# Expert tokens fetched as quarter rows and transposed on VectorE, stores of the residual stream moved into the router stage

## The reference

```python
h = rmsnorm(x, g_pre_ffn) * (1 + sc2) + sh2
aff = softmax(h @ w_router)                    # 16 experts
g, idx = lax.top_k(aff.T, cap)                 # cap = 64 latent tokens per expert, 16 context tokens
xe = h[idx]
hid = silu(xe @ w_gate[e]) * (xe @ w_up[e])    # 1024 -> 2816
ye = (hid @ w_down[e]) * g[..., None]          # 2816 -> 1024
out = zeros.at[idx].add(ye)
x = x + gt2 * rmsnorm(out, g_post_ffn)
```

## Time and profile before

| | us |
|---|---|
| median of three runs | 2022.64 (2022.20 to 2023.88) |
| profiled execution, its own time | 2023.81 |
| its span, first to last instruction | 2021.9 |
| PE busy | 1938.5 (96%) |
| DVE busy | 419.7 (21%) |
| ACT busy | 263.4 (13%) |
| POOL busy | 137.8 (7%) |
| bytes moved by DMA | 643.85 MB |

### The profile page before, as it was taken

How to read it: one execution, slowest core, us unless ns; L and a number is a source line. 1 busy time by engine, 2 the same in 40 slices (tenths; PEclk the granted TensorE clock), 3 DMA queues, 4 the chain that set the end, 5 groups by cost and what they waited for, 6 DMA issues and landing times.

```text
span 2021.9 us, 36578 instructions
## 1 busy us (share of the span) xinstructions
PE 1938.5 (96%) x16672; PEld 885.9 (44%) x16672; DVE 419.7 (21%) x759; ACT 263.4 (13%) x507; POOL 137.8 (7%) x208
## 2 busy tenths in 40 slices
PE   6999999999948999999999999999999999999994
PEld 3889778775842333333333333333333333333331
DVE  2432355535260111011101111011101110111013
ACT  4222345432210000000000000000000000000001
POOL 1000000000110000010000100000100000100012
PEclk9999999999968999999999999999999999999997
DMA  9751111122059999999999999999999999999993
GB/s 393 269 191 61 45 47 57 40 77 110 32 214 401 413 413 412 413 403 414 413 412 409 409 409 412 410 410 412 413 404 409 413 409 413 404 408 413 421 388 141
DMA packets 103331, 643.85 MB, mean 318 GB/s; under 512 B 11776, under 2 KB 15248, under 8 KB 45584
## 3 DMA queue, kind: packets, MB, share of 16 engines
q1 hardware_dynamic: 96384, 624.39, 76.0%
q0 software_dynamic: 6800, 17.18, 3.1%
HBM read 625.00 MB, written 16.52 MB: 317 GB/s over the span
## 4 chain that ended last, share of the span: by engine, by line
PE 94%; DMA 2%; DVE 2%; issue 1%; SPq 0%; ACT 0%; POOL 0%; POOLq 0%; DVEq 0%; ACTq 0%
PE ps L806 92%; DMA slab_x<-in_w_mod_blocks 1%; PE ps L975 1%; DMA zgB<-gg_dram 1%; PE ps L1205 1%; PE ps L894 0%; DVE topi L1800 0%; PE ps L1106 0%; PE ps L839 0%; DVE topv L1799 0%; DVE work L1802 0%; DVE Gs L1645 0%; DMA xe<-xn_dram,idx_g 0%; PE ps L1005 0%; DVE fin L1927 0%
## 5 line engine op out<-in xcount | busy, mean ns | idle before, releaser
L806 PE MATMUL ps<-ring,xeT 128*32 128x512 f32 (+1 forms) x9216 | 920.9, 559 | 5.3 <-DVE hid L1884 3.3
L806 PEld LDWEIGHTS ps<-ring,xeT 128*32 128x32 f32 x9216 | 298.9, 110 | 621.6 <-issue 615.2
L806 PE MATMUL ps<-ring,hidT 128*32 128x512 f32 x4224 | 467.7, 595 | 11.6 <-DVE hidT L1891 11.6
L806 PEld LDWEIGHTS ps<-ring,hidT 128*32 128x32 f32 x4224 | 135.7, 110 | 319.3 <-issue 305.5
L1884 DVE TENSOR_TENSOR hid<-sil,ps 128x768 f32<-128x768 f32 (+1 forms) x48 | 42.6, 887 | 1106.6 <-ACT sil L1475 1106.6
L1475 ACT ACTIVATE sil<-ps 128x768 f32<-128x768 f32 (+1 forms) x48 | 36.3, 757 | 1154.6 <-PE ps L806 1154.6
L806 PE MATMUL ps<-hT_hi,gq_hi 128*128 128x320 f32 x256 | 88.1, 344 | 0.0
L806 PE MATMUL ps<-in_hi,hT_hi 128*128 128x384 f32 x240 | 82.2, 343 | 0.0
L806 PE MATMUL ps<-in_lo,hT_hi 128*128 128x384 f32 x240 | 80.4, 335 | 0.0
L806 PE MATMUL ps<-in_hi,hT_lo 128*128 128x384 f32 x240 | 80.3, 335 | 0.0
L806 PE MATMUL ps<-hT_hi,gq_lo 128*128 128x320 f32 x256 | 79.1, 309 | 0.0
(11 more groups left out here) (233 smaller groups left out, 1226.3 us busy)
## 6 DMA issues: line engine op xcount, KB each, us to landing
ring<-in_w_gu SPq DMA_DIRECT2D x256, 1024.0 KB, 15.9
ring<-in_w_dn SPq DMA_DIRECT2D x176, 1024.0 KB, 18.2
ring<-in_w_gu_rest SPq DMA_DIRECT2D x128, 768.0 KB, 21.3
slab_y<-in_w_mod_blocks SPq DMA_DIRECT2D x8, 2048.0 KB, 8.6
in_slab<-in_w_in_blocks SPq DMA_DIRECT2D x6, 1536.0 KB, 8.9
gq<-in_w_gates SPq DMA_DIRECT2D x16, 512.0 KB, 3.4
slab<-in_w_mod_blocks SPq DMA_DIRECT2D x3, 2048.0 KB, 15.7
x<-in_x_sample SPq DMA_DIRECT2D x8, 512.0 KB
```

What stands on the lines that cost most here:

```text
L806: return pe.matmul(out, lhsT, rhs, start=first, stop=last, **kw)
```

## The change

**Rows and gathers.** `xn_dram` becomes 2560 rows of 256 values: a quarter x of a token's row holds the columns f*128 + x*32 + c of all eight f. ACT writes this order into the new tile `xq` with one scaled copy (`quarters`), and POOL stores `xq`. An expert's rows come by three gathers of 128 quarter rows (1 KB each), for the two halves of the latent tokens and for the context tokens, which are fetched twice over. The index tables `fG` and `idxT` have three columns for each expert, built by 12 DVE instructions ahead of `top_ready` and turned by three PE transposes.

**Transposes.** `tokens_T` on PE goes. DVE's `transpose` turns the 32 by 32 squares of `xe` into `xs`, and the multiplication reads `xs`. It covers 96 columns, so the zeroing of columns 80 to 95 goes too.

**Order.** `residual` of the last tile comes after the first round of `choose`, and `scaled`, `h2_low`, `l_max` and `affinity` of that tile go from rounds 0, 1, 3, 4 to 2, 3, 5, 6. The stores of `x1` go from SP, after the ring loads, to POOL, one behind each `xn_dram` store. At the end the pair matrices and two PE matmuls go: DVE copies half of the sums to the other partitions and adds (`both_halves`), and POOL takes the mean.

```diff
-            for t in range(NT):
-                dst = x1_dram[2 * t * P:2 * (t + 1) * P, :].rearrange("(p n) d -> p (n d)", n=2)
-                sp.dma_start(dst, x1[:, home(t), :]).then_inc(x1_stored, 16)
...
-                pool.wait_ge(x2_ready, i + 1)
-                pool.dma_start(xn_dram[t * P:(t + 1) * P, :], row[i % 2][:, :]).then_inc(x2_stored[i % 2], 16)
+                pool.wait_ge(xq_ready, i + 1)
+                dst = xn_dram[4 * t * P:4 * (t + 1) * P, :].rearrange("(p x) d -> p (x d)", x=4)
+                pool.dma_start(dst, xq[i % 2][:, :]).then_inc(x2_stored[i % 2], 16)
+                dst = x1_dram[2 * t * P:2 * (t + 1) * P, :].rearrange("(p n) d -> p (n d)", n=2)
+                pool.dma_start(dst, x1[:, home(t), :]).then_inc(x1_stored, 16)
...
             def gather():
-                pool.indirect_dma_start(xe[:, :], None, xn_dram[:, :],
-                                        bass.IndirectOffsetOnAxis(ap=idx_g[:, :], axis=0)).then_inc(gathered, 16)
+                for g in range(3):
+                    pool.indirect_dma_start(xe[:, g, :], None, xn_dram[:, :],
+                                            bass.IndirectOffsetOnAxis(ap=idx_g[g][:, :], axis=0)).then_inc(gathered, 16)
...
-            def tokens_T(e):
-
-                pe.wait_ge(gathered, val(e, 16, 16))
-                for k in range(KD):
-                    last = pe.transpose(ps[:, 6 + k // 4, (k % 4) * CT:(k % 4 + 1) * CT], xe[:, k * P:(k + 1) * P],
-                                        par[0:CT, 0:CT])
-                last.then_inc(xeT_done, 1)
...
+            def quarters(i):
+                act.wait_ge(x1_rs, i + 1)
+                if i >= 2:
+                    act.wait_ge(x2_stored[i % 2], 16 * (i // 2))
+                dst = xq[i % 2][:, :].rearrange("p (x f c) -> p f x c", x=4, f=KD)
+                src = x1[:, home(LATE[i]), :].rearrange("p (f x c) -> p f x c", f=KD, x=4)
+                act.activation(dst, src, ACT.Copy, scale=rs2[:, i:i + 1]).then_inc(xq_ready, 1)
...
+            for x in range(4):
+                dve.tensor_scalar(fG[:, 0:2, x, :], topi[:, 0:CL].rearrange("e (g j) -> e g j", g=2), 4.0, float(x),
+                                  ALU.mult, ALU.add)
+                for n in range(2):
+                    last = dve.tensor_scalar(fG[:, 2, x, CC * n:CC * (n + 1)], topi[:, CL:CT], 4.0, float(4 * LAT + x),
+                                             ALU.mult, ALU.add)
+            link(last)
+            dve.sem_inc(top_ready, 1)
...
             def tokens_scaled(e):
-                dve.wait_ge(xeT_done, val(e, 1, 1))
+                dve.wait_ge(gathered, val(e, 48, 48))
+                if not is_first(e):
+                    dve.wait_ge(x_mul, val(e, 2, 0))
+                dve.transpose(xs[:, :, :].rearrange("p g d -> p (g d)"), xe[:, :, :].rearrange("p g d -> p (g d)")).then_inc(
+                    xs_ready, 1)
+                dve.wait_ge(xs_ready, val(e, 1, 1))
+                for c, (g0, g1) in enumerate(((0, 2), (2, 3))):
+                    src = xs[:, g0:g1, :].rearrange("p g (f j) -> p f g j", f=KD)
+                    dst = xeT[:, :, 32 * g0:32 * g1].rearrange("p f (g j) -> p f g j", j=32)
+                    gain_ = A2[:, c, :].unsqueeze(2).unsqueeze(3).to_broadcast([P, KD, g1 - g0, 32])
+                    dve.tensor_tensor(dst, src, gain_, ALU.mult).then_inc(x_mul, 1)
...
+            def both_halves(n, m):
+                dve.wait_ge(f_sq, NT + n + 1)
+                dve.tensor_copy(ssw[0:m, n:n + 1], ssz[m:2 * m, n:n + 1])
+                link(dve.tensor_copy(ssw[m:2 * m, n:n + 1], ssz[0:m, n:n + 1]))
+                dve.tensor_tensor(rsz[0:2 * m, n:n + 1], ssz[0:2 * m, n:n + 1], ssw[0:2 * m, n:n + 1], ALU.add).then_inc(z_sum, 1)
```

More of the change, by code:

```diff
@@ L225, in program @@
         row = [at(f"row{i}", B0 + 8192 + i * 4096, [P, D]) for i in range(2)]
+        xq = [at(f"xq{i}", 98304 + i * 4096, [P, D]) for i in range(2)]
         h2T = [at(f"h2T{i}", B0 + 16384 + i * 4096, [P, KD, P]) for i in range(2)]
@@ L301, in program @@
         work_c = small("work_c", [E_, CTX])
-        idxT = small("idxT", [CT, E_], I32)
-        idx_g = small("idx_g", [CT, 1], I32)
+        idxT = small("idxT", [P, 3, E_], I32)
+        idx_g = [small(f"idx_g{g}", [P, 1], I32) for g in range(3)]
         assert SB0 + S0[0] <= 229344, S0[0]
@@ L730, in scatter, with first_rows @@
                                             compute_op=ALU.add).then_inc(scattered, 16)
[L732 to L736, removed]
+            def first_rows(e):
+                for g in range(3):
+                    pool.tensor_copy(idx_g[g][:, :], idxT[:, g, e:e + 1]).then_inc(idxg_set, 1)
+                pool.wait_ge(idxg_set, 3 * e + 3)
+                gather()
+            first_rows(0)
+            pool.wait_ge(gathered, 48)
             pool.sem_inc(router_gone, 1)
[L738 to L741, removed]
+            pool.wait_ge(xs_ready, 1)
+            first_rows(1)
             pool.wait_ge(tab_set, 1)
@@ L745, in _ @@
             with pool.Fori(0, E_ - 2) as e:
-                pool.wait_ge(xeT_done, e + 2)
+                pool.wait_ge(xs_ready, e + 2)
                 pool.sem_inc(pool_turn, 1)
-                pool.tensor_copy(idx_g[:, :], idxT[:, bass.ds(e + 2, 1)]).then_inc(idxg_set, 1)
-                pool.wait_ge(idxg_set, e + 3)
+                for g in range(3):
+                    pool.tensor_copy(idx_g[g][:, :], idxT[:, g, bass.ds(e + 2, 1)]).then_inc(idxg_set, 1)
+                pool.wait_ge(idxg_set, e * 3 + 9)
                 pool.sem_inc(pool_turn, 1)
@@ L788, in _ @@
             for n, p in enumerate((P, 64)):
-                pool.wait_ge(z_mean, n + 1)
-                pool.tensor_tensor(rsz[0:p, n:n + 1], rsz[0:p, n:n + 1], mhalf[0:p, :], ALU.pow).then_inc(f_rs, 1)
+                pool.wait_ge(z_sum, n + 1)
+                z = rsz[0:p, n:n + 1]
+                link(pool.tensor_scalar(z, z, 1.0 / D, EPS, ALU.mult, ALU.add))
+                pool.tensor_tensor(z, z, mhalf[0:p, :], ALU.pow).then_inc(f_rs, 1)
             pool.wait_ge(out_stored, 16 * NT)
@@ L1147, in _ @@
             pe.wait_ge(top_ready, 1)
-            pe.transpose(ps[0:CT, 5, 0:E_], topf[:, :], par[0:E_, 0:E_]).then_inc(topT_done, 1)
+            for g in range(3):
+                last = pe.transpose(ps[:, 5, g * E_:(g + 1) * E_], fG[:, g, :, :].rearrange("e x j -> e (x j)"),
+                                    par[0:E_, 0:E_])
+            last.then_inc(topT_done, 1)
             pe.transpose(ps[0:2 * KD, 4, 0:P], GG2[:, :, :].rearrange("p c k -> p (c k)"), ident)
@@ L1460, in _ @@
                     l_exp(i - 2)
+                quarters(i)
             h2_high(NT - 2)
@@ L1465, in _ @@
             x1_square(NT - 1)
+            quarters(NT - 1)
             h2_high(NT - 1)
@@ L1823, in _ @@
                 if r == 0:
+                    residual(NT - 1)
+                if r == 2:
                     scaled(NT - 1)
-                if r == 1:
+                if r == 3:
                     h2_low(NT - 1)
-                if r == 3:
+                if r == 5:
                     l_max(NT - 1)
-                if r == 4:
+                if r == 6:
                     affinity(NT - 1)
@@ L1848, in _ @@
             dve.wait_ge(topT_done, 1)
-            dve.tensor_copy(idxT[:, :], ps[0:CT, 5, 0:E_]).then_inc(idx_ready, 1)
+            dve.tensor_copy(idxT[:, :, :], ps[:, 5, 0:3 * E_].rearrange("p (g e) -> p g e", g=3)).then_inc(idx_ready, 1)
             dve.wait_ge(tabT_done, 1)
@@ L1936, in _ @@
             turned(last, 1)
-            for pair, m in ((pairA, 64), (pairB, 32)):
-                for n in range(2):
-                    p = 2 * m
-                    pairs = dve.tensor_tensor(pair[:, n * m:(n + 1) * m], ident[0:p, 0:m], ident[0:p, m:p], ALU.add)
-            link(pairs)
             for t in range(2):
@@ L1960, in _ @@
             dve.scalar_tensor_tensor(yrB[0:64, :], yb[:, :], gB[:, e:e + 1], yrB[0:64, :], ALU.mult, ALU.add).then_inc(z_ready, 1)
-            def mean(n, p, bank):
-                dve.wait_ge(pair_done, n + 1)
-                dve.tensor_scalar(rsz[0:p, n:n + 1], ps[0:p, bank, 0:1], 1.0 / D, EPS, ALU.mult, ALU.add).then_inc(z_mean, 1)
+            def both_halves(n, m):
[3 more added lines that the diff above has]
+                dve.tensor_tensor(rsz[0:2 * m, n:n + 1], ssz[0:2 * m, n:n + 1], ssw[0:2 * m, n:n + 1], ALU.add).then_inc(z_sum, 1)
             def finished(n, p, z, zg, zx):
@@ L1969, in finished @@
                                          ALU.add).then_inc(f_ready, 1)
-            mean(0, P, 5)
+            both_halves(0, 64)
             link(dve.tensor_tensor(zgA[:, :], yrA[:, :], zgA[:, :], ALU.mult))
+            both_halves(1, 32)
             finished(0, P, yrA, zgA, zxA)
-            mean(1, 64, 0)
             dve.wait_ge(z_ready, 3)
```

41 lines of the change are left out of this document (14 added, 27 removed).

## The result

The changed kernel takes 2010.11 us (median of five runs, 2008.87 to 2013.68) against 2022.64 us for the kernel before, timed beside it: 0.9939 of its time, 95% interval 0.9929 to 0.9950. It is 12.5 us faster, where I had forecast 5 us slower and a range down to 2015. The profiled execution took 2008.87 us with a span of 2007.1, 14.8 us less than the span of before.

What follows compares the result with a forecast made beforehand. The prediction took the DMA engines, through the late landing of the gain rows, as the bound, not PE. Terms +3.9 - 6.3 + 7.5 + 0.1 = +5.2 us on 2022.64 gave 2027.8 us, range 2015 to 2044.

Steps and rivals of the forecast that it cites:

- The gathers: Expert stage: the new gathers cost the ring's DMA stream +0.5 us an expert, +7.5 us for fifteen.
- the lower bound: Expert stage: a new gather loses nothing beyond its 0.94 us of bytes, 0.7 us an expert less than before.
- The rival with +1.9 for two more DMAs: Expert stage: each DMA or row has its own price, +1.5 to +1.9 us an expert, 2043 to 2050 us; chance 0.12.
- the bytes rival: Expert stage: bytes alone set the gather's price, 0 to 0.3 us more each, 2020 to 2025 us; chance 0.24.
- The stores of x1: SP's queue after the last ring load: moving five 512 KB stores to POOL brings the gain rows 6.3 us earlier.
- G: End of the kernel: the landing of the gain rows, 1988.80 us before, which releases finish(0) and sets the end.
- The start of load 9: Router stage: the first ring load after the first gathers starts 3.9 us later (3 to 6), and the gain rows with it.
- So everything after 1988.8 hangs on that landing: End of the kernel: the last 33.1 us follow the landing of the gain rows, and PE has idled before them.
- the rival's floor: Faster rival, cheap short-row gathers: PE's place sets the end, -6.7 us, 2016 us, hardly better; chance 0.22.
- the two clocks: Expert stage: PE's work and the lagging DMA engines run side by side, and the DMA engines set the end.
- PE's 10.6 us: Expert stage: without token transposes PE saves 15 x 0.71 us, but waits for the gain rows; cost and gain 0.
- The tail: End of the kernel: POOL does one more small instruction for each half, +0.1 us, between -0.5 and +0.7.

Runs made afterwards that it cites:

- b_x1pool: The kernel before with its five stores of x1 moved from SP to POOL in the router stage: 2015.61 us, 0.9963.
- b_128: The kernel before with each gather of 80 rows of 4 KB filled up to 128 with dummy rows: 2015.11 us, 0.9961.
- a_96: The changed kernel with each gather fetching 96 of its 128 quarter rows, the last quarter of every token left out: 2019.35 us, 0.9982.
- b_112: The kernel before with each gather of 80 rows of 4 KB filled up to 112 with dummy rows: 2029.48 us, 1.0035.
- a_x1sp: The changed kernel with the stores of x1 put back on SP behind the ring loads: 2017.27 us, 0.9970.
- b_rows1k: The kernel before with its 80 rows fetched as four gathers of 80 quarter rows of 1 KB: 2028.17 us, 1.0023.

## Why the prediction was wrong, point by point

**The gathers: the step that failed.** "I take +0.5, near the price by bytes" gave +7.5 us for 15 gathers; they brought about -10. At 419 GB/s undisturbed, an old gather loses (419 - 377) x 10 / 419 = 1.0 us beside its own 0.78, a new one (419 - 412) x 10 / 419 = 0.17 beside 0.94. The change is -0.67 us an expert, the lower bound that I had named ("nothing lost at all, 0.94, that is 0.7 us an expert less than now") and put aside. The table agrees: 192 KB more for each gather are 15 x 0.47 = +7 us, and the 128-row gather still brought -8, so 15 us belong to the dents.

Two readings led there. I took the scatter as the nearest row because its loss per byte was the old gather's. But the scatter's loss is in its own packets: over the 732 to 738 us stretch of before, its queue takes 29.8% of the engines' time for 0.33 MB (87 us for one MB), while the ring's MB costs 39.8 us, near the undisturbed 38.5. The gather's loss is mostly in the ring's packets: (42.7 - 38.5) x 2.65 = 11 us of engine time in the window above, against (50.8 - 38.5) x 0.33 = 4 in its own. The mean rate of a window can't tell these apart; the queues' bytes and shares in the same window do, and they stood in the trace of before. And I compared row lengths, rows and DMAs, but never partitions, though the change goes from gathers over 80 to gathers over 128.

The Trainium skill (DMA: Bandwidth & Descriptors, The descriptor swizzle) says that in a transfer over 128 partitions each DMA engine writes the partitions of one port of SBUF, and points to another rule for other shapes. If a gather is split like that transfer, one over 128 partitions keeps every engine on the port that its ring packets use, and one over fewer might not; which ports it would use the section doesn't say. The condition found here fits such a cause, with 64 to 112 rows alike. That ports are the cause is not shown, as no trace here shows a port.

**The price of each DMA.** The rival with +1.9 for two more DMAs fell too. My estimate of 0.8 us for each came from the Trainium skill (DMA: Bandwidth & Descriptors, Measured), which has 0.95 us for 64 KB and calls transfers under 64 KB dominated by their descriptors. These gathers move 128 KB each, and all three cost 0.17 us beyond their bytes, so a fixed part of a lone transfer is not what it takes from a stream beside it. The packets came as the bytes rival counted them. POOL's queue has 80, 96 and 144 of them in the window behind one gather of 64, 80 and 128 rows, so 16 beyond the rows; for the three gathers of the changed kernel it has 144, which leaves 96, or 6 for each engine against 5.

**The stores of x1** (-6.3): right, -6.3 and -7.5 in the two runs (6.1 and 6.9 for G). Their price on PE, 2.5 us in the last expert, I didn't have; here G hides it. **The start of load 9** (+3.9): +3.0 measured, inside my 3 to 6.

**"So everything after 1988.8 hangs on that landing"**: right before and after. But the rival's floor, "then the saving on PE counts: -6.7, 2016 us", was wrong by my own rows. PE had already idled 11.6 us there, so its place would only set the end when G came 11.6 us further forward than PE: at -6.7 - 11.6 = -18.3 us. G moved by -2.6 + 3.0 - 7 - 10 = -16.6 (16.9 measured) and stayed the later of the two clocks. "It can't be much better" cut the range where the time then fell.

**PE's 10.6 us**: the sum of the pieces of 0.71 us was 2.0 us too small. The period of 85.85 us was on record, but not what it would be without them; it is 85.00. This changed nothing in the forecast, as G sets the end.

**The tail** (+0.1): three small terms. The first store comes 0.6 us later after PE's end, in my range. The last 72 matmuls take 9.3 us instead of 10.6: after 11.6 us of idle time the granted clock was 0.75 over them, after 5.1 us 0.86, and in `b_x1pool`, after 1.0 us, 1.00 (8.0 us). Beyond 1.0 us the length of the idle time doesn't order them: 10.6 us after 6.9 (`b_128`), 9.7 after 14.3 (`a_96`), 9.3 after 17.5 (`b_112`). So of the 1.3 us between the two profiles I can't say what the change earned and what is luck. And the program ends 10.8 us after the start of the last store instead of 8.0, a term that I didn't have (below).

By these terms the medians should differ by +3.0 - 7 - 10 + 0.6 - 1.3 + 2.75 = -12 us; they differ by -12.5. The -7 is that of the stores in G, and with the uncertain 1.3 the agreement is closer than the terms are known.

## What to carry to other kernels

When a stream keeps all DMA engines busy, try an indirect gather into SBUF beside it over all 128 partitions, with dummy rows if need be (plain transfers weren't tried), and read in a window which queue's packets became slower, not only the total rate. When two clocks run side by side, write down how long the earlier one already waits before you say where it takes over. What waits for a late landing shouldn't stand in an in-order program ahead of work that the busiest engine needs.

## What the runs showed of the hardware that I had not expected

A gather of 64, 80, 96 or 112 rows beside a saturated stream costs it the same 1.0 us on top of the gather's bytes, and one of 128 rows nothing (375 to 377 against 419 GB/s). With 1 KB rows and 96 partitions (`a_96`) the loss was smaller, 387 GB/s.

POOL's last instruction, the drain at the end of the program (duration in ns, start in us), took 2.75 us longer, before and then after:

```profile
L171 POOLq DRAIN  x1: 9610/9610/9610, 2012.0 to 2012.0; - x1
```

```profile
L171 POOLq DRAIN  x1: 12356/12356/12356, 1994.5 to 1994.5; - x1
```

Its length goes with the number of DMAs that POOL has issued, not with their bytes: 84 DMAs in the kernel before 9.61 us, 84 with 128-row gathers 9.61, 89 in `b_x1pool` 10.02, 116 in `a_x1sp` 12.24, 121 in the changed kernel 12.36, 132 in `b_rows1k` 12.95. That is 3.34 us for 48 more, 0.07 us each on average and not evenly (five more cost 0.41 us in one pair and 0.12 in another), paid at the end of the program.

Left open: why packets slow down beside a gather on fewer partitions; why PE has gaps in the last expert once the stores of `x1` are on POOL; and why the same 1.9 us of idle time before the output projection is followed within 3 us by a stretch at half the full clock in four of the sixteen profiled executions and by none in the others.
